# Two norms of a fused transformer kernel: the projections behind them begin on the unnormed residual, and the attention's gate columns share a weight block

## The reference

```python
def rmsnorm(x, g):
    xf = x.astype(jnp.float32)
    y = xf * lax.rsqrt(jnp.mean(xf * xf, axis=-1, keepdims=True) + EPS)
    return (y * g.astype(jnp.float32)).astype(x.dtype)

def modulate(h, shift, scale):
    return h * (1 + scale[:, None, :]) + shift[:, None, :]
...
        x = x + gate1[:, None, :] * (y @ w_out[i])

        h2 = modulate(rmsnorm(x, norm2_g[i]), shift2, scale2)
        g_ff, up_ff = jnp.split(h2 @ w_ffn_in[i], 2, axis=-1)
        x = x + gate2[:, None, :] * ((jax.nn.silu(g_ff) * up_ff) @ w_ffn_out[i])

    shift_f, scale_f = jnp.split(c_act @ ada_f_w + ada_f_b, 2, axis=-1)
    return modulate(rmsnorm(x, norm_f_g), shift_f, scale_f)
...
    proj = h @ w_in
...
    fq, fk, fv, ff, nq, kc, vc, ks, vs, kw, vw, ng = [proj[..., offs[i]:offs[i + 1]] for i in range(len(IN_SIZES))]
    hd = (B, S, FOX_HEADS, HEAD_DIM)
    log_f = jax.nn.log_sigmoid((ff + b_f).astype(jnp.float32))
```

## Time and profile before

| | us |
|---|---|
| median of 3 runs | 1792.05 |
| lowest and highest | 1791.80, 1792.96 |
| the profiled execution | 1791.37 |
| its span | 1789.7 |
| PE busy | 1690.9 (94%) |
| DVE busy | 915.0 (51%) |
| ACT busy | 659.7 (37%) |

### The profile page before, as it was taken

How to read it: one execution, slowest core, us unless ns; L and a number is a source line. 1 busy time by engine, 2 the same in 40 slices (tenths; PEclk the granted TensorE clock), 3 DMA queues, 4 the chain that set the end, 5 groups by cost and what they waited for, 6 DMA issues and landing times.

```text
span 1789.7 us, 22284 instructions
## 1 busy us (share of the span) xinstructions
PE 1690.9 (94%) x8263; PEld 1328.3 (74%) x8263; DVE 915.0 (51%) x1368; ACT 659.7 (37%) x944; POOL 172.4 (10%) x182
## 2 busy tenths in 40 slices
PE   2999889999999989999998999999999899999996
PEld 1657667888888877666667788888887688888885
DVE  6865584553343353656557644444336744444223
ACT  1324334444322252545554444443225333333221
POOL 5001107940000020000000000002000000000000
PEclk9999889999999989999999899999999799999998
DMA  8664054533332232111102222233222032223221
GB/s 287 211 197 165 25 187 156 179 124 102 104 99 97 81 105 72 47 37 43 42 12 83 71 94 94 96 104 114 97 66 77 26 102 96 94 94 117 97 80 47
DMA packets 48730, 179.78 MB, mean 100 GB/s; under 512 B 5984, under 2 KB 6656, under 8 KB 48416
## 3 DMA queue, kind: packets, MB, share of 16 engines
q1 hardware_dynamic: 44896, 166.75, 27.8%
q0 software_dynamic: 2624, 10.59, 2.0%
q10 hardware_dynamic: 1152, 1.66, 0.3%
HBM read 173.56 MB, written 2.10 MB: 98 GB/s over the span
## 4 chain that ended last, share of the span: by engine, by line
PE 66%; issue 23%; DVE 8%; ACT 2%; DMA 1%; POOL 1%; ACTq 0%; DVEq 0%; POOLq 0%; SPq 0%
PE bank L335 15%; PE bank L337 15%; PE bank L336 15%; PE bank L1252 3%; PE bank L1254 2%; PE bank L1253 2%; PE bank L1316 2%; PE bank L1360 2%; PE bank L1336 2%; PE bank L1086 1%; DVE ada_acc L1724 1%; DVE w_lo L274 1%; PE bank L1416 1%; DMA raw<-in_ada_w 1%; PE bank L429 1%
## 5 line engine op out<-in xcount | busy, mean ns | idle before, releaser
L274 DVE TENSOR_TENSOR w_lo<-raw,w_hi 128x1024 fp32r<-128x1024 f32 (+1 forms) x236 | 322.1, 1365 | 622.0 <-ACT w_hi L270 621.8
L335 PE MATMUL bank<-h_hi,w_hi 128*128 128x512 f32 x1232 | 488.0, 396 | 6.1 <-DVE h_lo L534 2.7
L337 PE MATMUL bank<-h_hi,w_lo 128*128 128x512 f32 x1232 | 481.7, 391 | 0.0
L336 PE MATMUL bank<-h_lo,w_hi 128*128 128x512 f32 x1232 | 481.6, 391 | 0.0
L270 ACT ACTIVATE w_hi<-raw 128x1024 fp32r<-128x1024 f32 (+1 forms) x236 | 265.4, 1125 | 550.9 <-PE bank L337 477.1
L335 PEld LDWEIGHTS bank<-h_hi,w_hi 128*128 128x128 f32 x1232 | 232.3, 189 | 65.1 <-issue 7.1
L337 PEld LDWEIGHTS bank<-h_hi,w_lo 128*128 128x128 f32 x1232 | 232.5, 189 | 49.2
L336 PEld LDWEIGHTS bank<-h_lo,w_hi 128*128 128x128 f32 x1232 | 232.5, 189 | 47.5 <-issue 1.0
L335 PE MATMUL bank<-hid_hi,w_hi 128*128 128x512 f32 x528 | 205.6, 389 | 0.0
L336 PE MATMUL bank<-hid_lo,w_hi 128*128 128x512 f32 x528 | 205.4, 389 | 0.0
L337 PE MATMUL bank<-hid_hi,w_lo 128*128 128x512 f32 x528 | 205.4, 389 | 0.0
(11 more groups left out here) (334 smaller groups left out, 1929.7 us busy)
## 6 DMA issues: line engine op xcount, KB each, us to landing
raw<-in_f2i SPq DMA_DIRECT2D x88, 512.0 KB, 3.2
raw<-in_ffi SPq DMA_DIRECT2D x44, 512.0 KB, 3.3
raw<-in_f2o SPq DMA_DIRECT2D x32, 704.0 KB, 4.1
ada_w<-in_ada_w SPq DMA_DIRECT2D x32, 512.0 KB, 4.0
raw<-in_att_w SPq DMA_DIRECT2D x24, 512.0 KB, 3.3
raw<-in_ffo SPq DMA_DIRECT2D x16, 704.0 KB, 4.0
raw<-in_ada_w SPq DMA_DIRECT2D x16, 512.0 KB, 5.0
raw<-in_w_in SPq DMA_DIRECT2D x16, 512.0 KB, 5.3
```

Of the source, the lines that this page charges most:

```text
L274: nc.vector.tensor_tensor(WL[par][:, 0:kc * P], RAW[s][:, 0:kc * P], WH[par][:, 0:kc * P].bitcast(F32), ALU.subtract).then_inc(wlo, 1)
L335: pe_.matmul(bank[:, :], w_h, hi[:, k0 + k, :], start=start and k == 0, stop=False)
L336: pe_.matmul(bank[:, :], w_h, lo[:, k0 + k, :], start=False, stop=False)
L337: last = pe_.matmul(bank[:, :], w_l, hi[:, k0 + k, :], start=False, stop=stop and k == kc - 1)
```

## The change

It has three parts.

*Up projection of the first feed-forward (`ffi0`).* Its blocks 0 and 1 are multiplied on x·gain, without the token's scale. ACT writes the high halves (`LH`) and DVE the low halves (`LL`, `lead_low`) behind each `w_out` block. `pe_phase_led` takes the place of `pe_phase`: the norm's last sums stand inside the first lead block, behind its third chunk. W^T·shift comes from 16 products of two columns behind each of these blocks (`shift_sums`: the shift's high and low part, by w_hi and by w_lo). The token's scale is broadcast a second time into `PS[3]`, ACT copies it, and DVE scales the two banks (`lead_scaled`). Blocks 2 and 3 are multiplied side by side, three chunks apart, on the normed chunks. The rows and turn of modulation vector 5 go behind them. The vectors of the modulation are ordered differently in memory (`MOD_ORDER`), and `ada_turn(4)` stands behind `w_out` block 6 and no longer behind block 7.

*The attention's first projections (`att5`).* Forget gates and NSA gates are one block (columns 0 to 7 and 32 to 55), so there are seven. The first two blocks, the gates' and the first keys', are multiplied on x·gain (`GL`, of both norms), held in `HH` and `FLL`; ACT and DVE write them in `ffo0`. Since the normed chunks go to the same `HH`, ACT waits for `f_step`, which the second lead block bumps chunk by chunk. The sums for the attention's norm stand between the two lead blocks. Blocks 3 and 4 are multiplied side by side, then block 5 and the rest.

*Attention loop (`att6`).* `stage` moves to slots 13 to 15 of the iteration before; the weights' low parts are written one slot behind a block's evacuation (`att_split`).

```diff
+
+            def shift_sums(t):
                 if t == 0:
-                    behind_first()
+                    pe_.wait_ge(lead_sh, 2)
+                for k in range(C):
+                    for e, w in enumerate((WH[t], WL[t])):
+                        m = pe_.matmul(PS[2][:, 2 * t:2 * t + 2], w[:, k * P:(k + 1) * P], SHL[:, k, :],
+                                       start=t == 0 and k == 0 and e == 0, stop=t == 1 and k == C - 1 and e == 1,
+                                       skip_group_check=True)
+                return m
+            for t in range(2):
+                pe_.wait_ge(ev[t], cnt)
+                pe_.wait_ge(wlo, n + t + 1)
+                for k in range(C):
+                    if t == 0:
+                        pe_.wait_ge(lead_lo, k + 1)
+                    part(t, t, LH, LL, k)
+                    if t == 0 and k == 2:
+                        inside_lead()
+                shift_sums(t).then_inc(mm, 1)
+                if t == 0:
+                    behind_lead()
+            for step in range(C + LAG):
+                if step < C:
+                    if step == 0:
+                        pe_.wait_ge(ev[0], cnt + 1)
+                        pe_.wait_ge(wlo, n + 3)
+                    pe_.wait_ge(n_lo, ready + step + 1)
+                    m = part(0, 0, hi, lo, step)
+                    if step == C - 1:
...
                     ada_rows(4, ada_used, C * 3)
-                if n == C - 1:
+                if n == C - 2:
                     ada_turn(4)
...
+            for e, w in enumerate((1, 0)):
+                pe_.wait_ge(ev[w], cnt5 + e)
+                pe_.wait_ge(wlo, n5 + e + 2)
+                for k in range(C):
+                    if e == 0:
+                        pe_.wait_ge(f_lo, k + 1)
+                    m = att_part(w, FLL, k)
+                    if e == 1:
+                        m.then_inc(f_step, 1)
+                    if e == 0 and k == 3:
+                        pe_bcast(nj["nf"])
+                        pe_.matmul(PS[3][:, :], ONE[:, :], DG, start=True, stop=True).then_inc(f_rb, 1)
+                if e == 0:
+                    pe_.wait_ge(f_sh, 2)
+                for k in range(C):
+                    for half, w_ in enumerate((WH[w], WL[w])):
+                        m = pe_.matmul(PS[2][:, 2 * e:2 * e + 2], w_[:, k * P:(k + 1) * P], FSH[:, k, :],
+                                       start=e == 0 and k == 0 and half == 0, stop=e == 1 and k == C - 1 and half == 1,
+                                       skip_group_check=True)
+                m.then_inc(mm, 1)
+                if e == 0:
+                    pe_sum_cross(nj["q0"], 0)
+            for step in range(C + LAG):
+                if step < C:
...
+                    m = att_part(1, HL, step)
+                    if step == C - 1:
+                        m.then_inc(mm, 1)
+                if step >= LAG:
+                    if step == LAG:
+                        pe_.wait_ge(ev[0], cnt5 + 2)
+                        pe_.wait_ge(wlo, n5 + 5)
+                    m = att_part(0, HL, step - LAG)
+                if step == C - 1:
+                    pe_bcast_next(nj["q0"])
+            m.then_inc(mm, 1)
...
                 act.activation(X[:, k, :], TMP[:, k % 2, :], ACT.Identity, bias=MOD[:, 48 + k:49 + k]).then_inc(xs[0], 1)
+                act.wait_ge(f_step, k + 1)
                 act.activation(HH[:, k, :], TMP[:, k % 2, :], ACT.Identity, bias=GS[:, 0, k:k + 1],
                                scale=vcol("norm_g2", k)).then_inc(n_hi, 1)
+                if k == 0:
+                    act.wait_ge(f_rb, 1)
+                    act.activation(FK[0][:, :], PS[3][:, :], ACT.Copy).then_inc(f_rf, 1)
+                if k == 2:
+                    split_hi(N0["att5"] + 3, 1, 3, C, ROUND["att5"])
+            split_hi(N0["att5"] + 4, 0, 0, C, ROUND["att5"] + 1)
...
                     split_lo(N0["w_out"] + n + 2, n % 2, (n + 2) % 4, C)
+                for k in {C - 3: (0, 1), C - 2: (2, 3), C - 1: (4, 5, 6)}.get(n, ()):
+                    if k == 0:
+                        dve.wait_ge(mod_ready, 6)
+                    lead_low(k)
+                if n == C - 1:
+                    dve.wait_ge(ada_sum, 5)
+                    dve.tensor_tensor(MOD[:, 32:40], PS[5][:, 32:40], VEC[:, COL["ada_b"] + 32:COL["ada_b"] + 40],
+                                      ALU.add).then_inc(mod_ready, 1)
...
+                    dve.wait_ge(f_bias, 1)
+                    dve.wait_ge(ev[1], O0["att5"] // 2 + 1)
+                    dve.scalar_tensor_tensor(LX, FQ[1][0:NH, :], FBI[0:NH, 0:1], RQ0[0:NH, :], ALU.add,
+                                             ALU.mult).then_inc(f_lx, 1)
+                    dve.scalar_tensor_tensor(NG, FQ[1][32:32 + 3 * NH, :], FBI[32:32 + 3 * NH, 0:1],
+                                             RQ0[32:32 + 3 * NH, :], ALU.add, ALU.mult).then_inc(f_ng, 1)
                     dve.wait_ge(ld_small, 16 * 3)
...
                     dve.tensor_tensor(dst[:, :], PS[t % 2][:, :], RQ0, ALU.mult).then_inc(ev[t % 2], 1)
-                split_lo(N0["att6"] + j + 2, t % 2, (t + 2) % 4, C)
+
+            def att_split(j):
+                split_lo(N0["att6"] + j + 2, j % 2, (j + 2) % 4, C)
...
                         if sl == 7:
                             out_lo(it, 0)
+                    if p < 4 and sl >= SLOTS - 3:
+                        if p:
+                            dve.wait_ge(a6["sc"], 2 * NP_ * p)
+                        if p and sl == SLOTS - 1:
+                            dve.wait_ge(a6["nm"], 2 * NP_ * p)
+                        stage(p, (sl - SLOTS + 4) % 3)
                     for j in ready_at.get((p, sl), ()):
                         att_block(j)
+                    for j in ready_at.get((p, sl - 1) if sl else (p - 1, SLOTS - 1), ()):
+                        att_split(j)
             out_lo(3, 1)
 
```

323 lines of the change are left out of this document (241 added, 82 removed).

## The result

The changed kernel took 1807.17 us (median of 4 runs, 1805.63 to 1808.00), the kernel before in the same comparison 1792.51. The ratio is 1.0086, with a 95% interval of 1.0074 to 1.0099: 15.4 us slower by the ratio, 14.7 by the medians. The direction and the three places of the forecast hold, the size does not: 1800.9 was forecast, with 1806.5 as the upper end.

The account below looks back on a forecast made before the run. TensorE (PE), busy 94% of the span, was taken as the bound. 1.0 + 12.6 - 4.8 = +8.8 us on the profiled 1791.37 gave 1800.2, and 0.7 for the median 1800.9 us; range 1791.0 to 1806.5.

Parts of the forecast that it names:

- The second part: `att5`: one block saved, but new pauses and clock losses; +12.6 us, range +4.6 to +14.3.
- The pauses: `att5`: PE waits 7.8 us at the pair's second block and 7.0 us ahead of block 5.
- four falls of the clock: `att5`: up to four clock losses, behind the norm's pause, tiny products and both new pauses; 2.0 us each, 8.0 added.
- The third part: Attention loop: PE's wait for DVE's scores at L1304 goes, with half a clock loss; -4.8 us, between -2 and -7.5.
- The first part: w_out's end to `ffi0`'s fourth block: 1.5 us less at full clock, one clock loss taken; +1.0, between -1.5 and +3.4.
- The modulation rows and turns: `ffi0`, behind the normed chunks: no longer hidden in DVE's norm, they add 1.4 us, with 0.3 of slack.
- stand only w_out's own products: w_out: behind PE's new wait of about 3.9 us ahead of block 7 come only w_out's own products.
- the chunk chain keeps up: Rival in `att5`: DVE's last w_lo is there by 654.7, neither pause comes; time about 1778; chance 0.05.
- the clock stays up: Rival: no clock losses, `ffi0` -1.5, `att5` +4.6, attention loop -4.8; 1790.4 us; chance 0.13.
- small products at 0.041 each: Rival: two-column products cost 0.041 us, not 0.115; 4.7 us less, partly refilled by waits; 1797; chance 0.08.
- the attention part gives nothing: Rival in the attention loop: another wait on the same DVE queue follows; 1805.7 us; chance 0.12.
- More falls of the clock than counted: Rival: more clock falls, with tiny products at 0.22 us each in them; above 1806 us; chance 0.07.

Follow-up runs that it names:

- e3: Changed kernel with ACT's copy of modulation vector 5 moved ahead of the hidden chunk's operations: 1800.39 us, ratio 1.0055 to the kernel before.
- e2: Changed kernel with its first part (`ffi0` lead blocks, place of vector 4's turn, vector order) taken back: 1799.46 us, ratio 1.0054 to the kernel before.
- e4: Changed kernel with another order on ACT and DVE behind `att5`'s pair of blocks: 1797.04 us, ratio 1.0037 to the kernel before.
- e6: Changed kernel without its first part and without lead blocks in `att5`; merged gates and loop part kept: 1781.37 us, ratio 0.9945 to the kernel before.
- e1: Kernel before with the attention loop's part alone (`stage` in slots 13 to 15, w_lo one slot later): 1786.07 us, ratio 0.9976.
- e5: e3 with the turn of vector 4 put back behind w_out's block 7: 1800.60 us, ratio 1.0055 to the kernel before.
- e9: e6 plus first part, vector 5's copy early, vector 4's turn behind block 7, low halves 4 to 6 behind last residual: 1779.12 us, ratio 0.9932.

## Why the forecast was right in its direction and short in its size

**The second part, +12.6 forecast, +12.3 in the trace.** Point by point, with the 6.6 us by which it started late taken off: lead 0 at 633.5 (forecast 633.5), the mean at 633.3 (633.3), lead 1 at 646.1 (644.7; the clock was at half in lead 0, which the full-clock sum had left out), the first low half at 647.9 (646.3), the last w_lo's end at 663.5 (662.5), block 5 at 682.5 (678.5 at full clock). The pauses were 5.6 for 7.8 and 7.5 for 7.0; the first is shorter because PE came later to it, by the clock. All four falls of the clock came. The forecast took 2.0 each, because parts of them fall where PE would wait anyway. e3 shows that one inside lead 1 costs nothing: without it the pause behind is 7.2 us and not 5.6. e2 shows that this depends on the place, since a fall that begins ahead of lead 1 moves the first low half. The 6 us at half clock behind the second pause cost 3.0. So the nearness of the two sums is in part luck: where the clock falls differs between profiles, and with it the stretch by up to 2.6 us. e4 and e6 confirm the causes: the order behind the pair cost 10.5 us, and without the lead blocks the merged gates are worth 4.7, so that the lead blocks in `att5`, even in the better order, cost 6.4 (52.1 against 45.7). That the normed chunks overwrite what lead 1 reads is ACT's wait of 6.61 us in the trace; no run gives them a tile of their own, so how much of the 6.4 this is stays open.

**The third part, -4.8 forecast, -5.7 in the trace**, in e1 as in the changed kernel. The waits went in full; of the clock's fall half was counted, and all of it went.

**The first part, +1.0 forecast, +8.5 in the trace.** Here the forecast failed, and at one step: "The modulation rows and turns, no longer hidden in DVE's norm, 1.4, with 0.3 of slack". It counted what PE issues. Between the rows and the turn stands a copy by ACT, for which the forecast has no term, and the change put it behind the hidden chunk's operations on ACT, which wait for DVE. (The text on the kernel before knows of DVE's copy only.) It cost 5.3 us of wait and, since the clock fell behind it, 2.4 more. e3 removes the copy's delay alone, and 6.7 of these 7.7 us go. The 0.3 of slack that the forecast left stands where 7.7 were needed. The rest of the first part's sum was near: the wait ahead of block 7 is 3.6 (3.9), with the start shifted by 1.9 the last residual is at 259.7 (258.7), the lead blocks end at 277.5 (274.6, at full clock), the pair at 289.2 (286.6). The 2.5 us of the fall behind the first wait account for most of both differences; the forecast had added one such loss at the end.

In the same part the forecast said that behind the new wait for vector 4's turn "stand only w_out's own products". That reading was right for PE, but e5 shows that taking this wait out alone gains nothing: DVE's low halves ahead of the last residual then set the time, but for 1.3 us. Only with them moved too (e9) did the stretch fall. A pause that is seen on PE is not yet its price.

**The sum.** 6.3 us separate the medians, 1807.2 and 1800.9. The first part missed by 7.5, the rest of the program added 1.0, and the median lies 1.5 above the profiled execution where 0.7 were taken. The second and third part (1.2 together) and the head (1.9) went the other way. Without the head's 1.9, which is not put down to the edit, the forecast would have been further off.

**The rivals.** That the chunk chain keeps up is refuted by the two pauses; that the clock stays up by the rows at 0.50; small products at 0.041 each by the starts 0.111 apart; that the attention part gives nothing by e1. More falls of the clock than counted was right in part: one more, in `ffi0`, and it came with a wait that was not in the sum; its small products at 0.22 each did not come.

## What to carry to other kernels

When an instruction pair is moved on the engine that sets the time, look at what stands between the two on the other engines, and where that now is in their queues: the copy between a product and its use has a place of its own. Blocks that start ahead of a norm hide its latency only if nothing they read is overwritten by what comes after it; here the normed chunks had to wait for the second lead block, and DVE's chain of 15.5 us (654.53 to 670.07) was moved behind its start rather than beside lead 0. This is read from the trace; a kernel without the overwriting was not run. Of a change with three parts, build each alone: the merged gates and the loop's order were worth 10 us, and hidden under the order of two queues (6.7 and 10.5 us in the stretches) and the lead blocks of `att5` (6.4).
